# SSD scan of a hybrid encoder: y formed channel-major, carried states scaled by broadcast rows

## Chip, cores, metric

One core of a Trainium2 chip. The metric is the device time of one execution in microseconds (us). A lower time is better. The engines are TensorE (PE), VectorE (DVE), ScalarE (ACT), GpSimd (POOL) and SyncE (SP).

## What is computed

Two layers over 512 positions of width 1024 in float32: a bidirectional Mamba-2 SSD layer, then differential attention. The change lies in the scan of the first. It has 32 heads of 64 channels in 8 groups of 4 heads, a state of 128 per group, and 4 chunks of 128 positions:

```python
# per direction; xin = x * dt; C, B: (chunk, position, group, state)
L = where(lower triangle, exp(a_cs[l] - a_cs[s]), 0)
y_diag = einsum('bclgn,bcsgn,bgrcls,bcsgrp->bclgrp', C, B, L, X)
states = einsum('bcsgn,bgrcs,bcsgrp->bcgrpn', B, exp(a_cs[-1] - a_cs), X)
# scan over chunks: new = carry * exp(a_cs[-1]) + states; prev = the carry that each chunk receives
y_off = einsum('bclgn,bcgrpn,bgrcl->bclgrp', C, prev, exp(a_cs))
y = y_diag + y_off          # both directions are added, then
y = y + x * d_skip
y = rmsnorm(y * silu(z)) @ w_out
```

## The kernel before

The input projection is cut into units: one unit gives 128 output columns for all 512 positions, in 24 matmuls (`project`, L1290). Each iteration of the SSD stage has six slots, one unit each: slots 0 and 1 give z of scan group g, slots 2 and 3 give xT (the two 128-channel halves, two heads each), slot 4 BT and slot 5 CTr of group g + 1. Units alternate between banks 0 and 1, and `project` waits until the SiLU of the unit two before it is done (`silu_done`). Beside its unit, each slot carries a piece of the scan of group g. Groups 2 to 5 run in a hardware loop (two trips of two groups), the others are written out.

Every engine runs its instructions in the order written. The pieces for group g are, by slot:

- slot 0: PE transposes xT into banks 2 and 3 (L1309), ACT copies them to `x_nat` (position-major).
- slot 1: PE transposes BT and forms the products of B and C (bank 5). DVE forms the pair weights (`rows`, L967, L971): for each head and chunk the matrix of C, B and the decays of both directions.
- slot 2: PE forms the chunk states (L1333); DVE chains them into `prev` (L981, L987) and signals `prev_done`.
- slot 3: PE forms the within-chunk part: 16 matmuls per group with `rows` stationary and 64 columns of `x_nat` moving (L1344), then the part from the carried states: six matmuls with a chunk of CTr stationary and 256 columns of `prev` moving (L1357). DVE scales the second by `eacs` = exp(a_cs), one value per position (on partitions) and head (L1002), and adds both directions (L1008, L1011); y stands position-major in `x_nat`.
- slot 5: PE transposes y back to channels (L1364, eight 128x128 transposes); DVE adds the D skip (L1018), multiplies by the gate zT (L1021) and signals `g_done`.

In the last group, slot 3's carried-state work is spread over slots 3 and 4, and units of the output projection run in slots 2 to 5.

Within a slot DVE runs `conv` (four taps, L942), then the scan piece, then `silu` (L957), for slots 2 to 5. ACT runs, in a slot, `split_hi` of a later unit's weights (L612), `evacuate` (L654 or L650), scan copies and exponentials (L705), and `tanh` (L661) once `conv` is done. POOL forms `w_lo` (L471), masks `rows` (L503), scales x into `x_dec` (L492). SP loads the weights.

The order within a slot on DVE, which the change does not alter, is:

```python
                    if slot in slots and slot >= 2:
                        conv(m, half, slot)
                    if scan and slot < 5:
                        scan_ops(m * 2 + half, slot, half)
                    if slot in slots and slot >= 2:
                        silu(m, half, slot)
```

`Own` (L251) makes DVE wait for the instruction just issued, because the next one reads its result.

Of the kernel before, what the change touches and what calls it, by code (L numbers as in the profile page):

```python
# [23 lines left out]
F32 = mybir.dt.float32  # L24
# [99 lines left out]
def build(nc, x, norm_w, ssd_w_in, ssd_conv_w, ssd_conv_b, ssd_dt_bias, ssd_a_log, ssd_d,  # L124
# [3 lines left out]
    with stack:  # L128
# [3 lines left out]
        def sem(name):  # L132
# [30 lines left out]
        tmp = sb("tmp", [P, 2 * GW], F32, ssd)  # L163
        sq_acc = sb("sq_acc", [P, L], F32, ssd)
# [37 lines left out]
        acs_rows = nc.dram_tensor("acs_rows", (2 * HEADS, L), F32).ap()  # L202
        bias_rows = nc.dram_tensor("bias_rows", (AH, 2 * L), F32).ap()
# [22 lines left out]
        y_done, yt_done, g_done, sq_in, sq_done = (  # L226
            sem("y_done"), sem("yt_done"), sem("g_done"), sem("sq_in"), sem("sq_done"))
# [90 lines left out]
        def scan_banks(g):  # L318
# [18 lines left out]
        def load_rows(queue, g):  # L337

            after(queue, diag_done, g * 2)
# [9 lines left out]
        def _(sp):  # L349
# [37 lines left out]
            for n in range(UNITS_O1):  # L387
                if n == 8:
                    sp.wait_ge(diag_done, 2 * GROUPS)
# [214 lines left out]
        def _(act):  # L604
# [66 lines left out]
            def scan_ops(g, slot, half):  # L671
                if slot == 0:

                    after(act, y_done, g * NC)
                    after(act, yt_done, g * 2)
# [7 lines left out]
                if slot == 2:  # L683
                    act.wait_ge(st_done, g * 3 + 1)
                    after(act, off_done, g * NC)
                    nc.scalar.copy(pair(0), bank[scan_banks(g)[0][0]][:, :]).then_inc(prev0_in, 1)
# [65 lines left out]
            nc.scalar.activation(flat(eacs), flat(acs), ACT.Exp).then_inc(sp_a, 1)  # L752
# [134 lines left out]
        def _(dve):  # L887
# [85 lines left out]
            def scan_ops(g, slot, half):  # L973
                if slot == 2:

                    after(dve, off_done, g * NC)
                    after(dve, y_done, g * NC)
                    dve.wait_ge(prev0_in, g + 1)
                    state = scan_banks(g)[0]
# [12 lines left out]
                if slot == 3 or slot == 4 and last_g:  # L992

                    for c in (range(NC) if not last_g else range(2) if slot == 3 else range(2, NC)):
                        d0, d1 = (1 if c == 0 else 0), (1 if c == NC - 1 else 2)
                        if c == 0:
                            dve.wait_ge(prev_done, g + 1)
                        else:
                            dve.wait_ge(y_done, g * NC + c)
                        dve.wait_ge(off_done, g * NC + c + 1)  # L1000
                        dve.wait_ge(diag_done, g * 2 + c // 2 + 1)
                        own(V.tensor_tensor(  # L1002
                            tmp[:, d0 * GW:d1 * GW].rearrange("p (d r n) -> p d r n", d=d1 - d0, r=HPG),
                            bank[scan_banks(g)[1][c]][:, d0 * GW:d1 * GW].rearrange("p (d r n) -> p d r n", d=d1 - d0, r=HPG),
                            eacs[:, c, d0:d1, ds(g * HPG, HPG)].unsqueeze(3)
                            .to_broadcast([P, d1 - d0, HPG, HD]), ALU.mult))
                        within = bank[6 + c // 2][:, (c % 2) * GW:(c % 2 + 1) * GW]
                        ins = V.tensor_tensor(x_nat[:, c, :], within, tmp[:, d0 * GW:(d0 + 1) * GW], ALU.add)  # L1008
                        if d1 - d0 == 2:
                            own(ins)  # L1010
                            ins = V.tensor_tensor(x_nat[:, c, :], x_nat[:, c, :], tmp[:, GW:2 * GW], ALU.add)  # L1011
                        ins.then_inc(y_done, 1)
                if slot == 5:

                    for j in range(2):
                        t = gT_flat[:, ds((g * 2 + j) * L, L)]
                        dve.wait_ge(yt_done, g * 2 + j + 1)
                        own(V.scalar_tensor_tensor(bank[6 + j][:, :], xT[:, half, j, :],  # L1018
                                                   par[:, ds(g * 2 + (PC_D + j), 1)], bank[6 + j][:, :],
                                                   ALU.mult, ALU.add))  # L1020
                        V.tensor_tensor(t, bank[6 + j][:, :], zT[:, j, :], ALU.mult).then_inc(g_done, 1)  # L1021
# [7 lines left out]
            def ssd_iteration(m, half, slots=range(SLOTS), scan=True):  # L1029
                for slot in range(SLOTS):  # L1030
# [18 lines left out]
                    if scan and slot == 5:  # L1049
                        scan_ops(m * 2 + half, slot, half)  # L1050
# [9 lines left out]
            dve.wait_ge(sp_a, 7)  # L1060
# [10 lines left out]
            OWN_V = 2 * (4 * (TAPS - 2) + 2 + 3 + 6 + 2)  # L1071
# [549 lines left out]
```

## Time and profile before

| | us |
|---|---|
| median of 3 runs | 892.61 (891.35 to 892.84) |
| the profiled execution | 891.45 |
| its span | 889.7 |

| engine | busy us | share of the span |
|---|---|---|
| PE | 793.6 | 89% |
| PE weight load | 641.8 | 72% |
| DVE | 562.5 | 63% |
| POOL | 476.5 | 54% |
| ACT | 404.5 | 45% |

The SSD stage lies from about 40 to 460 us of the span, the scan groups 0 to 7 from about 60 to 445. Behind them come the output projection, the attention heads and the last projection, which the change does not touch. The profile names a line (L1261 is the line of the projections' matmul, inside a helper), an engine, an operation, and what it writes and reads. Matmuls of plain float32 operands appear as two records each. A duration of a matmul includes its latency: neighbours overlap, so their cost is read from start to start.

### The profile page before, as it was taken

The numbers are of one execution on the slowest core, as the hardware profiler recorded it, in microseconds if no ns is written. First come the engines' busy times: TensorE is split into PE (matmuls) and PEld (weight loads), VectorE is DVE, ScalarE is ACT, GpSimd is POOL, SyncE is SP. The second block draws the span as 40 slices with busy tenths as digits, with TensorE's granted clock in tenths as the row PEclk, the third lists the DMA queues.
The fourth block names the chain that finished last, engine by engine and source line by source line (L and its number), as shares of the span: only waits on it lengthen the run. The fifth ranks groups of instructions, "written<-read, shape, count | busy, mean of one in ns | idle before, by whom it ended". The sixth has DMA issues, their size and how long they took to land.

```text
span 889.7 us, 11512 instructions
## 1 busy us (share of the span) xinstructions
PE 793.6 (89%) x3824; PEld 641.8 (72%) x3824; DVE 562.5 (63%) x885; ACT 404.5 (45%) x807; POOL 476.5 (54%) x270
## 2 busy tenths in 40 slices
PE   1988999999999999997999998989888797987787
PEld 1767888878888787886878886766666575766566
DVE  4755878785969596876620134667676867667643
ACT  4556473727272645556322343545434363544330
POOL 5439584947484757575454447536353554536121
PEclk9999999999999999999999999999999999999899
DMA  8133534342424233341523233232122212120002
GB/s 256 48 116 106 165 95 143 90 148 69 161 56 139 80 93 136 94 144 48 189 89 111 76 106 100 72 92 62 54 69 66 67 55 68 47 91 24 1 0 95
DMA packets 98772, 82.70 MB, mean 93 GB/s; under 512 B 4992, under 2 KB 87392, under 8 KB 96680
## 3 DMA queue, kind: packets, MB, share of 16 engines
q1 hardware_dynamic: 95728, 67.12, 25.2%
q10 hardware_dynamic: 2904, 15.01, 4.6%
q8 instruction: 24, 0.39, 0.2%
q14 instruction: 20, 0.16, 0.1%
q0 software_dynamic: 96, 0.02, 0.0%
HBM read 79.87 MB, written 2.26 MB: 92 GB/s over the span
## 4 chain that ended last, share of the span: by engine, by line
PE 46%; DVE 27%; issue 13%; ACT 6%; POOL 6%; DVEq 1%; DMA 1%; ACTq 0%; SPq 0%; POOLq 0%
PE bank L1261 39%; DVE c_acc L942 5%; DVE rows L967 4%; POOL stat L463 3%; DVE qkvz L1170 2%; DVE sbias L1131 2%; DVE tmp L1002 2%; ACT rows L705 1%; DVE x_nat L1011 1%; DVE x_nat L1008 1%; PE bank L1478 1%; DVE tmp L981 1%; DVE rows L971 1%; ACT ex L801 1%; DVE rows L903 1%
## 5 line engine op out<-in xcount | busy, mean ns | idle before, releaser
L471 POOL TENSOR_TENSOR w_lo<-w_raw,w_hi 128x1024 fp32r<-128x1024 f32 x104 | 261.9, 2520 | 226.5 <-ACT w_hi L612 226.3
L1261 PE MATMUL bank<-hn_hi,w_hi 128*128 128x512 f32 (+1 forms) x392 | 160.7, 410 | 11.6 <-DVE xT L957 8.9
L1261 PE MATMUL bank<-hn_hi,w_lo 128*128 128x512 f32 (+1 forms) x392 | 155.5, 397 | 0.0
L1261 PE MATMUL bank<-hn_lo,w_hi 128*128 128x512 f32 (+1 forms) x392 | 154.8, 395 | 0.0
L612 ACT CAST w_hi<-w_raw 128x1024 fp32r<-128x1024 f32 x104 | 108.7, 1046 | 74.8 <-PE bank L1261 68.7
L1261 PE MATMUL bank<-w_hi,hn_hi 128*128 128x512 f32 x320 | 134.3, 420 | 6.9 <-DVE zT L957 5.0
L1261 PE MATMUL bank<-w_hi,hn_lo 128*128 128x512 f32 x320 | 127.9, 400 | 0.0
L1261 PE MATMUL bank<-w_lo,hn_hi 128*128 128x512 f32 x320 | 127.8, 399 | 0.0
L801 ACT ACTIVATE ex<-sbias,stat 128x512 f32<-128x512 f32 x64 | 45.7, 715 | 159.1 <-DVE stat L1135 159.1
L942 DVE SCALAR_TENSOR_TENSOR c_acc<-bank,par,c_acc 128x510 f32<-128x510 f32 (+1 forms) x128 | 95.8, 748 | 32.0 <-ACT c_acc L654 23.3
L1261 PEld LDWEIGHTS bank<-hn_hi,w_hi 128*128 128x128 f32 (+1 forms) x392 | 74.5, 190 | 30.2 <-issue 15.2
L503 POOL TENSOR_TENSOR rows<-rows,below 128x1024 f32<-128x1024 f32 x32 | 76.6, 2420 | 23.1 <-DMA rows<-acs_rows 23.1
L1261 PEld LDWEIGHTS bank<-hn_hi,w_lo 128*128 128x128 f32 (+1 forms) x392 | 74.2, 189 | 16.8
L1261 PEld LDWEIGHTS bank<-hn_lo,w_hi 128*128 128x128 f32 (+1 forms) x392 | 74.6, 190 | 15.3
L1261 PEld LDWEIGHTS bank<-w_hi,hn_hi 128*128 128x128 f32 x320 | 62.3, 195 | 27.1 <-issue 10.6
L705 ACT ACTIVATE rows<-rows,da 128x128 f32<-128x128 f32 x256 | 78.0, 393 | 3.2 <-POOL rows L503 3.2
L661 ACT ACTIVATE bank<-c_acc 128x512 f32<-128x512 f32 x32 | 19.3, 602 | 119.2 <-DVE c_acc L942 119.2
L1261 PEld LDWEIGHTS bank<-w_hi,hn_lo 128*128 128x128 f32 x320 | 61.8, 193 | 13.8
L1261 PEld LDWEIGHTS bank<-w_lo,hn_hi 128*128 128x128 f32 x320 | 62.5, 195 | 11.5
L1261 PE MATMUL bank<-w_hi,oT_hi 128*128 128x512 f32 x128 | 52.5, 410 | 3.0 <-DVE oT_lo L1220 1.4
L967 DVE TENSOR_TENSOR rows<-rows 128x512 f32<-128x512 f32 x32 | 51.2, 1633 | 2.9 <-ACT rows L705 2.9
L463 POOL TENSOR_TENSOR stat<-stat,expo 128x16 f32<-128x16 f32 (+1 forms) x16 | 31.3, 1953 | 36.7 <-DVE stat L1181 19.0
(193 smaller groups left out, 1319.2 us busy)
## 6 DMA issues: line engine op xcount, KB each, us to landing
w_raw<-in_ssd_w_in SPq DMA_DIRECT2D x48, 512.0 KB, 4.0
w_raw<-in_attn_w_in SPq DMA_DIRECT2D x64, 256.0 KB, 3.1
rows<-acs_rows ACTq DMA_DIRECT2D x14, 1024.0 KB, 6.5
w_raw<-in_ssd_w_out SPq DMA_DIRECT2D x16, 512.0 KB, 3.6
w_raw<-in_attn_w_out SPq DMA_DIRECT2D x16, 256.0 KB, 3.1
wbias<-bias_rows SPq DMA_DIRECT2D x8, 448.0 KB, 4.1
rows<-in_x SPq DMA_DIRECT2D x4, 512.0 KB, 5.3
rows<-acs_rows SPq DMA_DIRECT2D x2, 1024.0 KB, 5.7
```

Source lines behind the costliest of these rows:

```text
L463: return nc.gpsimd.tensor_tensor(dst, src, expo[:, 0:n], ALU.pow)
L471: nc.gpsimd.tensor_tensor(w_lo[:, s, :], w_raw[:, s, :], f32(w_hi[:, s, :]), ALU.subtract)\
L503: nc.gpsimd.tensor_tensor(pair_, pair_, below[:, :, :].unsqueeze(2).to_broadcast([P, 2, NC, P]), ALU.add).then_inc(mask_done, 1)
L612: nc.scalar.copy(w_hi[:, s, :], w_raw[:, s, :]).then_inc(hi_done, 1)
L661: nc.scalar.activation(bank[u.c % 2][:, :], c_acc[:, u.c % 2, :], ACT.Tanh).then_inc(tan_done, 1)
L705: ins = nc.scalar.activation(part, part, ACT.Exp, bias=da[:, c, d, ds(g * HPG + r, 1)])
L801: nc.scalar.activation(ex[:, j, :], sbias[:, j, :], ACT.Exp, bias=stat[:, 36 + j:37 + j], accum_out=stat[:, 40 + j:41 + j]).then_inc(e_don ...
L942: ins = V.scalar_tensor_tensor(c_acc[:, p, lo:hi], bank[p][:, lo + sh:hi + sh], par[:, ds(t + (PC_W + k * CT), 1)], c_acc[:, p, lo:hi], AL ...
L967: ins = V.tensor_tensor(rows[:, r, :], rows[:, r, :], rows[:, HPG + r, :], ALU.add)
L1002: own(V.tensor_tensor(tmp[:, d0 * GW:d1 * GW].rearrange("p (d r n) -> p d r n", d=d1 - d0, r=HPG), bank[scan_banks(g)[1][c]][:, d0 * GW:d1 ...
L1131: ins = V.tensor_tensor_reduce(out=sbias[:, j, :], in0=bank[4 + j][:, :], in1=w, scale=1.0, scalar=-3.0e38, op0=ALU.add, op1=ALU.max, accu ...
L1261: ins = T.matmul(dst, a[i], b[j], start=first and n == 0, stop=last and n == 2)
```

## The change

The within-chunk part is formed channel-major: `x_nat` (64 channels of a head) is stationary and `rows` (128 positions) moves; the two heads of a half go to partitions 0 to 63 and 64 to 127 of bank 6 or 7. The carried-state part has `prev` stationary (128 channels) and a chunk of CTr moving, so it also comes out channel-major, 384 columns for each direction and half. exp(a_cs) must then vary along columns: ACT forms it once as rows, writes it to DRAM (`exp_rows`) and loads it for each group, broadcast to 64 partitions a head (`edec`, two transfers of 512 KB). The eight y transposes go, and `y_done` and `yt_done` with them. DVE's work on y, the D skip and the gate stand together in slot 4; in the last group, in slots 3 and 4.

```diff
+        edec = sb("edec", [P, 2, 2, L], F32, ssd)
...
+        exp_rows = nc.dram_tensor("exp_rows", (2, HEADS, L), F32).ap()
...
+        def off_part(g, n):
             if isinstance(g, int) and g == GROUPS - 1:
-                return (4, 6, 7), (4, 5, 4, 5)
-            return (4, 2, 3), (2, 3, 4, 5)
+                return n // 2, n % 2, bank[4 + n % 2]
+            return n % 2, n // 2, bank[(2, 4, 3, 5)[n]]
+
+        def off_cols(d):
+
+            return slice(P, L) if d == 0 else slice(0, L - P)
...
             def scan_ops(g, slot, half):
                 if slot == 0:
 
-                    after(act, y_done, g * NC)
-                    after(act, yt_done, g * 2)
+                    after(act, diag_done, g * 4)
...
+            def load_decay(g):
+
+                after(act, g_done, g * 2)
+                if isinstance(g, int) and g == 0:
+                    act.wait_ge(erows_out, 32)
+                for i in range(2):
+                    act.dma_start(edec[i * HD:(i + 1) * HD, :, :, :].rearrange("p j d l -> p (j d) l"),
+                                  exp_rows[i][ds(g * 4, 4), :].partition_broadcast(HD)).then_inc(edec_in, 16)
...
                     if scan and slot == 1 and not (isinstance(m, int) and m * 2 + half == 0):
                         squares(m * 2 + half - 1)
+                    if scan and slot == 1:
+                        load_decay(m * 2 + half)
...
-            nc.scalar.activation(flat(eacs), flat(acs), ACT.Exp).then_inc(sp_a, 1)
...
+            nc.scalar.activation(sq[0:2 * HEADS, 0, :], bank[5][0:2 * HEADS, :], ACT.Exp).then_inc(erows_sb, 1)
             act.wait_ge(rows_sb, 1)
             act.dma_start(acs_rows, tmp[0:2 * HEADS, :]).then_inc(rows_out, 16)
+            act.wait_ge(erows_sb, 1)
+            for d in range(2):
+                act.dma_start(exp_rows.rearrange("i (q d) l -> d q i l", d=2)[d],
+                              sq[d * HEADS:(d + 1) * HEADS, 0, :]).then_inc(erows_out, 16)
...
-                if slot == 3 or slot == 4 and last_g:
-
-                    for c in (range(NC) if not last_g else range(2) if slot == 3 else range(2, NC)):
...
-                if slot == 5:
-
                     for j in range(2):
...
+                if slot == 4 and not last_g:
+                    for j in range(2):
+                        from_states(g, 2 * j, tmp)
+                        from_states(g, 2 * j + 1, c_tan)
+                        within(g, j, half)
+                        add_states(g, 2 * j, tmp)
+                        add_states(g, 2 * j + 1, c_tan)
+                        gated(g, j)
+
+            def from_states(g, n, dst):
+
+                d, j, b = off_part(g, n)
+                cols = off_cols(d)
+                dve.wait_ge(edec_in, g * 32 + 32)
+                dve.wait_ge(off_done, g * 4 + n + 1)
+                V.tensor_tensor(dst[:, cols], b[:, cols], edec[:, j, d, cols], ALU.mult).then_inc(off_used, 1)
+
+            def within(g, j, half):
+
+                dve.wait_ge(diag_done, g * 4 + 2 * j + 2)
+                own(V.scalar_tensor_tensor(bank[6 + j][:, :], xT[:, half, j, :], par[:, ds(g * 2 + (PC_D + j), 1)],
+                                           bank[6 + j][:, :], ALU.mult, ALU.add))
+
+            def add_states(g, n, src):
+
+                d, j, _ = off_part(g, n)
+                cols = off_cols(d)
+                dve.wait_ge(off_used, g * 4 + n + 1)
+                own(V.tensor_tensor(bank[6 + j][:, cols], bank[6 + j][:, cols], src[:, cols], ALU.add))
+
+            def gated(g, j):
+
+                V.tensor_tensor(gT_flat[:, ds((g * 2 + j) * L, L)], bank[6 + j][:, :], zT[:, j, :], ALU.mult)\
+                    .then_inc(g_done, 1)
...
                     if slot in slots and slot >= 2:
                         silu(m, half, slot)
-                    if scan and slot == 5:
-                        scan_ops(m * 2 + half, slot, half)
...
                 if slot == 0:
 
                     pe.wait_ge(silu_done, g * SLOTS + 2)
-                    after(pe, y_done, g * NC)
+                    after(pe, off_used, g * 4)
...
                     pe.wait_ge(m_done, g * HPG + HPG)
                     if last_g:
                         pe.wait_ge(prev_done, g + 1)
...
                     for j in range(2):
                         for c in range(NC):
-                            ins = T.transpose(bank[6 + j][:, c * P:(c + 1) * P], x_nat[:, c, j * P:(j + 1) * P],
-                                              ident[:, :])
-                        ins.then_inc(yt_done, 1)
+                            for i in range(2):
+                                r = 2 * j + i
+                                ins = T.matmul(bank[6 + j][i * HD:(i + 1) * HD, c * P:(c + 1) * P],
+                                               x_nat[:, c, r * HD:(r + 1) * HD], rows[:, r, c * P:(c + 1) * P],
+                                               start=True, stop=True)
+                                if c == NC - 1:
+                                    ins.then_inc(diag_done, 1)
+                if slot == 3 or slot == 4 and last_g:
+
+                    pe.wait_ge(prev_done, g + 1)
+                    for n in range(4) if not last_g else range(2) if slot == 3 else range(2, 4):
+                        d, j, b = off_part(g, n)
+                        if slot == 4:
+                            pe.wait_ge(off_used, g * 4 + n - 1)
+                        for k in range(3):
+                            c = (k + 1, 2 - k)[d]
+                            ins = T.matmul(b[:, c * P:(c + 1) * P], prev[:, k, d, j * P:(j + 1) * P],
+                                           CTr[:, c * P:(c + 1) * P], start=True, stop=True)
+                        ins.then_inc(off_done, 1)
```

## Rows read from the trace of the kernel before

**Rows 1.** The page: busy us (share of the span) and instructions by engine.

```profile
PE 793.6 (89%) x3824; PEld 641.8 (72%) x3824; DVE 562.5 (63%) x885; ACT 404.5 (45%) x807; POOL 476.5 (54%) x270
```

**Rows 2.** The waits: engine, line, what it waited for; us in total, times, longest us.

```profile
PE bank L1261 <- DVE xT L957: 8.9, 7, 2.4
```

**Rows 3.** The timeline of PE, scan group 3: start us, us, engine, line, operation, count, idle before.

```profile
203.65 0.47 PE L1261 MATMUL bank<-hn_hi,w_hi 128*128 128x512 f32 x1
...
230.46 3.68 PE L1344 MATMUL bank<-x_nat,rows 128*128 128x64 f32 x32
233.97 2.81 PE L1357 MATMUL bank<-prev,CTr 128*128 128x256 f32 x12
236.43 0.58 PE L1261 MATMUL bank<-hn_hi,w_hi 128*128 128x512 f32 x1
...
243.57 0.47 PE L1261 MATMUL bank<-hn_hi,w_hi 128*128 128x512 f32 x1 [1.30 <-DVE xT L957]
...
249.14 1.03 PE L1364 MATMUL bank<-ident,x_nat 128*128 128x128 f32 x8
249.93 0.47 PE L1261 MATMUL bank<-hn_hi,w_hi 128*128 128x512 f32 x1
```

**Rows 4.** Stretch of slot 4's projection: length, busy us (count) by engine, clock, DMA.

```profile
236.43:242.11 5.68, 5.68 (x26) 4.49 (x24) 5.01 (x10) 1.65 (x2) 2.52 (x1) 1.00 0.98 342
```

**Rows 5.** The timeline of DVE, scan group 3.

```profile
232.11 0.69 DVE L987 TENSOR_TENSOR prev<-tmp,bank 128x512 f32<-128x512 f32 x1
...
236.66 0.41 DVE L1002 TENSOR_TENSOR tmp<-bank,eacs 128x256 f32<-128x256 f32 x1
...
242.74 0.68 DVE L957 SCALAR_TENSOR_TENSOR xT<-bank,c_acc 128x512 f32<-128x512 f32 x1
243.38 3.43 DVE L942 SCALAR_TENSOR_TENSOR c_acc<-bank,par,c_acc 128x510 f32<-128x510 f32 x4
```

**Rows 6.** The timeline of PE in attention: two matmuls of 64 rows each.

```profile
645.21 0.51 PE L1261 MATMUL bank<-qT_hi 64*128 64x512 f32 x2
```

**Rows 7.** The timeline of PE, last scan group, after its longest wait.

```profile
408.69 0.79 PE L1261 MATMUL bank<-w_hi,hn_hi 128*128 128x512 f32 x1 [4.96 <-DVE zT L957]
...
410.13 0.63 PE L1261 MATMUL bank<-w_hi,hn_hi 128*128 128x512 f32 x1
...
415.45 0.39 PE L1261 MATMUL bank<-w_hi,hn_lo 128*128 128x512 f32 x1
```

**Rows 8.** Groups by line and shape: count | busy us, mean ns | idle before.

```profile
L1002 DVE TENSOR_TENSOR tmp<-bank,eacs 128x512 f32<-128x512 f32 x16 | 11.1, 691 | 5.0 <-issue 3.3 <-DVE x_nat L1011 0.9
...
L1002 DVE TENSOR_TENSOR tmp<-bank,eacs 128x256 f32<-128x256 f32 x16 | 6.7, 420 | 3.1 <-PE bank L1357 2.4
```

**Rows 9.** The timeline of DVE: D skip and gate, in the loop, then written out.

```profile
208.84 0.75 DVE L1018 SCALAR_TENSOR_TENSOR bank<-xT,par,bank 128x512 f32<-128x512 f32 x1
209.73 0.69 DVE L1021 TENSOR_TENSOR gT<-bank,zT 128x512 f32 x1
...
394.93 0.74 DVE L1018 SCALAR_TENSOR_TENSOR bank<-xT,par,bank 128x512 f32<-128x512 f32 x1
395.71 0.69 DVE L1021 TENSOR_TENSOR gT<-bank,zT 128x512 f32<-128x512 f32 x1
```

**Rows 10.** The timeline of ACT, slot 4 of scan group 3.

```profile
242.46 0.78 ACT L654 ACTIVATE c_acc<-bank,par 128x512 f32<-128x512 f32 x1 [3.54 <-PE bank L1261]
```

**Rows 11.** The timelines of ACT's queue and of PE ahead of the first scan group.

```profile
58.63 0.55 ACTq L759 DMA_DIRECT2D acs_rows<-tmp  x1
...
82.48 2.86 PE L1333 MATMUL bank<-x_dec,B_nat 128*128 128x256 f32 x12 [3.02 <-POOL x_dec L492]
```

**Rows 12.** The timeline of PE: slot 4 of group 0, slot 0 of groups 1 and 7.

```profile
96.64 0.58 PE L1261 MATMUL bank<-hn_hi,w_hi 128*128 128x512 f32 x1
...
108.98 0.47 PE L1261 MATMUL bank<-hn_hi,w_hi 128*128 128x512 f32 x1
...
390.33 0.47 PE L1261 MATMUL bank<-hn_hi,w_hi 128*128 128x512 f32 x1
```

More of the change, by code:

```diff
@@ L337, in load_rows @@
         def load_rows(queue, g):
-            after(queue, diag_done, g * 2)
+            after(queue, diag_done, g * 4)
             if isinstance(g, int) and g == 0:
@@ L684, in scan_ops @@
                     act.wait_ge(st_done, g * 3 + 1)
-                    after(act, off_done, g * NC)
-                    nc.scalar.copy(pair(0), bank[scan_banks(g)[0][0]][:, :]).then_inc(prev0_in, 1)
+                    after(act, off_done, g * 4)
+                    nc.scalar.copy(pair(0), bank[state_banks(g)[0]][:, :]).then_inc(prev0_in, 1)
                 first = isinstance(g, int) and g == 0
@@ L974, in scan_ops @@
                 if slot == 2:
-                    after(dve, off_done, g * NC)
-                    after(dve, y_done, g * NC)
+                    after(dve, off_done, g * 4)
                     dve.wait_ge(prev0_in, g + 1)
-                    state = scan_banks(g)[0]
+                    state = state_banks(g)
                     for k in range(2):
@@ L991, in scan_ops @@
                 last_g = isinstance(g, int) and g == GROUPS - 1
-                if slot == 3 or slot == 4 and last_g:
-                    for c in (range(NC) if not last_g else range(2) if slot == 3 else range(2, NC)):
[L995 to L1012, printed above, removed]
@@ L1013, in scan_ops @@
-                if slot == 5:
-                    for j in range(2):
[L1016 to L1021, printed above, removed]
+                if slot == 3 and last_g:
+                    for j in range(2):
+                        from_states(g, j, (tmp, c_tan)[j])
+                    for j in range(2):
+                        within(g, j, half)
+                        add_states(g, j, (tmp, c_tan)[j])
@@ new lines, in scan_ops @@
+                if slot == 4 and last_g:
+                    for j in range(2):
+                        from_states(g, 2 + j, (tmp, c_tan)[j])
+                    for j in range(2):
+                        add_states(g, 2 + j, (tmp, c_tan)[j])
+                        gated(g, j)
+                if slot == 4 and not last_g:
+                    for j in range(2):
+                        from_states(g, 2 * j, tmp)
+                        from_states(g, 2 * j + 1, c_tan)
+                        within(g, j, half)
+                        add_states(g, 2 * j, tmp)
+                        add_states(g, 2 * j + 1, c_tan)
+                        gated(g, j)
@@ L1330, in scan_ops @@
                     for k in range(3):
-                        b = bank[scan_banks(g)[0][k]]
+                        b = bank[state_banks(g)[k]]
                         for d, (c, i) in enumerate(((k, k), (3 - k, 2 - k))):
@@ L1340, in scan_ops @@
                         pe.wait_ge(prev_done, g + 1)
-                    for c in range(NC):
-                        for r in range(HPG):
-                            at = (c % 2) * GW + r * HD
-                            ins = T.matmul(bank[6 + c // 2][:, at:at + HD], rows[:, r, c * P:(c + 1) * P],
-                                           x_nat[:, c, r * HD:(r + 1) * HD], start=True, stop=True)
-                        if c % 2:
-                            ins.then_inc(diag_done, 1)
+                    for j in range(2):
+                        for c in range(NC):
+                            for i in range(2):
[5 more added lines that the diff above has]
+                                    ins.then_inc(diag_done, 1)
@@ L1348, in scan_ops @@
                 if slot == 3 or slot == 4 and last_g:
                     pe.wait_ge(prev_done, g + 1)
-                    for c in (range(NC) if not last_g else range(2) if slot == 3 else range(2, NC)):
+                    for n in range(4) if not last_g else range(2) if slot == 3 else range(2, 4):
+                        d, j, b = off_part(g, n)
                         if slot == 4:
-                            pe.wait_ge(y_done, g * NC + c - 1)
-                        for d in range(2):
-                            k = (c - 1, 2 - c)[d]
-                            if 0 <= k < 3:
-                                ins = T.matmul(bank[scan_banks(g)[1][c]][:, d * GW:(d + 1) * GW], CTr[:, c * P:(c + 1) * P],
-                                               prev[:, k, d, :], start=True, stop=True)
-                        ins.then_inc(off_done, 1)
@@ L1360, in scan_ops @@
-                if slot == 5:
-                    pe.wait_ge(y_done, g * NC + NC)
-                    for j in range(2):
-                        for c in range(NC):
-                            ins = T.transpose(bank[6 + j][:, c * P:(c + 1) * P], x_nat[:, c, j * P:(j + 1) * P],
-                                              ident[:, :])
-                        ins.then_inc(yt_done, 1)
+                            pe.wait_ge(off_used, g * 4 + n - 1)
[3 more added lines that the diff above has]
+                                           CTr[:, c * P:(c + 1) * P], start=True, stop=True)
```

20 lines of the change are left out of this document (11 added, 9 removed).

## Prediction

> **What bounds the kernel now.** I read the page first: TensorE (PE) is busy 89% of the span, far ahead of VectorE (DVE) at 63% [rows 1]. A change that takes eight transposes a group off PE should therefore pay, unless it makes PE wait. So the second view is the list of waits: in the scan stage PE hardly waits, and its repeated wait is for DVE's SiLU of xT, 8.9 us in 7 times, the longest 2.4 [rows 2]. That wait shows the rule that decides here. `project` of a unit waits for `silu_done` of the unit two before it, because they share bank 0 or 1. In a slot DVE runs conv, then the scan work of that slot, then the SiLU, so scan work delays the release of the bank.
>
> Third, the timeline of PE over one trip of the loop (scan group 3), and those of DVE and ACT beside it. PE begins slot 0 at 203.65; within-chunk products run from 230.46, the products with carried states from 233.97, slot 4 from 236.43, slot 5 from 243.57, the y transposes from 249.14, and the next slot 0 starts at 249.93: a period of 46.28 us [rows 3]. Slot 4's projection takes 5.68 us, to 242.11 [rows 4]; so PE waits some 1.4 us before slot 5. DVE shows why: its y work of slot 3 starts at 236.66 and only at 242.74 does it reach the SiLU of slot 3; PE starts 0.83 us later [rows 3, 5]. This block sits in the slot where PE has most other work: between the ends of projections 3 and 4 it also has 5.97 us of scan products [rows 3], which hide nearly the whole block. In slot 4 DVE then has only the conv, from 243.38 [rows 5], and its SiLU, done well before PE wants bank 0 at 249.93. The remaining four instructions on y stand after the SiLU of slot 5 and delay no projection that is close.
>
> **Off PE.** The eight y transposes cost 249.14 to 249.93, 0.79 us a group [rows 3], 6.3 us in all. They matter only where PE is the last to be ready; after the change slot 0 waits for DVE (below), so in seven groups this is worth nothing and in the last 0.8 us.
>
> **Carried states on PE.** Six matmuls of 256 columns become twelve of 128: 1,536 columns either way. I take the same 2.46 us [rows 3].
>
> **Within-chunk products on PE.** Sixteen matmuls, each now with 64 stationary and 128 moving columns, two heads into the two halves of the output partitions. Today's take 3.51 us in 32 records, 0.110 each [rows 3]. The trace has no column halves. The nearest row is the one of row halves in the attention stage: two 64-row matmuls of 512 columns together cover 0.51 us, where one alone is recorded with 0.39, so they ran side by side [rows 6, 7]. If column halves do that too, the 16 matmuls cost half, about 1.8 us; if each waits for the other, some 3.4; if every change of half also cost the 0.11 by which slot 4's projection, which follows matmuls of another form, is longer than slot 5's [rows 3, 4], 5.2. I take 1.8, nearest to the only row with two halves. Not all of the 1.7 gained counts in the loop: the carried-state products also wait for `prev_done`, whose last instruction starts at 232.11 and takes 0.69 [rows 5], so they can start near 232.95 in place of 233.97: 1.0 us in each of the four groups in the loop, by my estimate up to 1.65 in the three written out, where DVE is faster, and 1.7 in the last. Sum: about 10 us.
>
> The Trainium skill, "TensorEngine Tiling (Array Packing)", section "Key Properties", says that different tiles run weight loads and matmuls in parallel. Its page "TensorE: Matmul & The Clock Gate", section "The mechanism", speaks against this change: there a weight load overlaps running matmuls only when the row group differs, and the two column halves have the same rows. By the first the products cost about 1.8 us, by the second about 3.4; the two matmuls of [rows 6] have different rows and so can't choose between them.
>
> **DVE's work on y.** Before, per group: four multiplications (two of 512 columns at 691 ns, two of 256 at 420 [rows 8]), six additions of 256, then twice a D-skip and a gating. After: four multiplications and four additions of 384 columns, and the same D-skips and gatings. 384 columns lie between the two forms, 0.555 us. What matters is that all twelve now stand in one block in slot 4 (groups 0 to 6), ahead of the SiLU of slot 4. Its length: an instruction that only follows another starts about 0.08 before the recorded end of the first, one that waits for its own result later. In the loop the D-skip starts at 208.84 and its gating at 209.73, so 0.89; written out, 394.93 and 395.71, so 0.78 [rows 9]. Per half of the channels, in the loop: two multiplications 2 x 0.55, D-skip 0.89, two additions with such waits 2 x 0.70, gating 0.65: 4.04, so 8.1 for the block. Written out: 2 x 0.50 + 0.78 + 2 x 0.60 + 0.61 = 3.6, so 7.2. An addition that reads and writes PSUM is not in the trace; the D-skip does both, in 0.75 for 512 columns, which bounds it, and nothing makes it cheaper than the 0.42 that a 256-column multiplication takes [rows 8, 9]: the block lies between 6.3 and 9.
>
> **The new path from the end of projection 4 to the next slot 0.** ACT evacuates from 242.46, an evacuation takes some 0.8, so DVE's conv of slot 4 starts no earlier than 243.2 (1.1 us behind PE's 242.11) and takes 3.43, 3.36 to the start of the next instruction. Then come the block, 8.1, and the SiLU with PE's start, 0.83 [rows 5, 10]. Sum 13.4 us in the loop and 12.1 where the code is written out (its three waits inside the conv are each 0.11 shorter, as 0.89 against 0.78 [rows 9]). PE itself has only slot 5's projection, 5.57 us, to do in that time [rows 3]: it stands still some 7 us in each of groups 0 to 6. Nothing hides this, since PE runs its projections in order. DVE is meanwhile idle from the SiLU of slot 3, about 238.1, until conv 4. The stall of 1.4 us ahead of slot 5 goes, but what is late next is later still. DVE's conv of slot 5 and ACT's tanh and exps behind it are also pushed back, but by as much as PE's next slot 0, so they add nothing.
>
> **The clock.** The wait of 4.96 us at 408.69 is followed by a unit that starts at half the clock: instructions of 0.63 in place of 0.39, and its 24th matmul starts at 415.45; with one more step of 0.23 the unit took 6.99 us, where 5.57 is usual [rows 3, 7]. A 7 us wait should do the same in each of seven iterations: +1.42 us each.
>
> **Added transfers.** ACT issues two broadcasts of 512 KB a group in slot 1, behind the squares, and waits for `g_done`, which the squares wait for as well. Two issues hold ACT's queue for about 1 us, at 0.55 for the one at 58.63 [rows 11], ahead of the split and evacuation of slot 2. I cost them at nothing, since DVE is then still at the pair weights of slot 1 and PE at the projection of slot 2; without that cover they would be 1 us a group, 8 in all. The data is first read in slot 4, more than 20 us on. Ahead of the first group ACT gets one more exponential of 64x512 and two issues, each like the 0.55 at 58.63 [rows 11], and loses one smaller exponential: some +1.4 us. PE's wait of 3.02 at 82.48 for POOL's x_dec [rows 11] hangs on this chain through the split weights, so I count it whole.
>
> **The sum.** Slot 0 of groups 1 and 7 start at 108.98 and 390.33: six periods of 46.9 on average [rows 12]. New period without a gain from column halves: 38.46 (203.65 to 242.11) + 1.42 + 13.4 = 53.3 in the four groups of the loop, 38.46 + 1.42 + 12.1 = 52.0 in the two written out. 4 x 53.3 + 2 x 52.0 = 317.2, less 281.35: +35.8. Group 0 begins slot 4 at 96.64: 96.64 + 5.68 + 12.1 = 114.4 against 108.98, +5.4 [rows 12]. Last group: +1.42 - 0.79 = +0.6. Ahead of the scan +1.4. Together +43.2. Column halves give back 10: +33.2. The profiled execution took 891.45 (span 889.7), 1.2 below the median of 892.61; 891.45 + 33.2 = 924.7, and on the median 925.8. I forecast 926.
>
> **The rivals.**
> Column halves take turns: everything else stands, 892.6 + 43.2 = 936. For it: today the products are paced by something other than 64 moving columns, since 0.110 a record of 64 columns is more than the 0.099 of a transpose of 128 (0.79 for eight [rows 3]). Against: [rows 6]. Chance 0.33.
> The stall is there but cheaper: half clock in only some iterations, or a block of 6.3: 917 to 922. Chance 0.07.
> Dearer than both: additions into PSUM at 9 us a block, or a settling time at each change of half, 941 to 950. Chance 0.07.
> Faster: the cut on PE decides. This needs the DVE block in slot 4 to be short enough to hide under slot 5's projection. The point is a block of about 4.2 us: 37.4 to the end of projection 4, 5.3 around the block, 46.9 today. If it were wholly hidden, transposes 6.3, stalls 8.9 [rows 2] and column halves 13.6 would go and 1.4 come: 865. Against: twelve instructions in 4.2 us are 0.35 each, and even 256 columns take 0.42 [rows 8]. Faster 0.02, no difference 0.01.
> My forecast has 0.50. Two measurements of this kernel can't be told apart below about 0.2%, 1.8 us. So faster 0.02, same 0.01, slower 0.97. The range 917 to 941 takes in the second and third case and most doubt on the block.
>
> **What would show it.** PE's waits should name DVE's SiLU of BT (slot 4) with about 7 us, seven times, and no longer xT. Slot 0 should begin with 0.63 us matmuls. The DVE timeline should show 7 to 8 us of y work between conv and SiLU of slot 4. The within-chunk products should take 1.8 us and the carried ones start right behind `prev_done`. I am wrong if DVE's block is under 4 us, if slot 0 starts within a microsecond of the end of slot 5, or if the attention stage changes length at all.

## The result, and the profile after

| | before | after |
|---|---|---|
| median, us | 892.35 (891.35 to 892.84) | 925.94 (923.53 to 926.24) |
| profiled execution, us | 891.45 | 926.24 |
| its span, us | 889.7 | 923.9 |

The changed kernel is slower: ratio 1.0372, with a 95% interval of 1.0352 to 1.0392. The page of after: its busy times, where [rows 1] stand for before, and its row of granted clock in tenths, with that of before below it:

```profile
PE 791.4 (86%) x3856; PEld 634.1 (69%) x3856; DVE 529.0 (57%) x869; ACT 406.2 (44%) x807; POOL 469.6 (51%) x270
...
PEclk9998999898989899898899999999999999998899
```

```profile
PEclk9999999999999999999999999999999999999899
```

PE does as much as before, 791.4 us against 793.6, in a span that is 34.2 us longer. DVE even lost 33.5 us of busy time. So the engines did not get more to do; PE stood still. The row of the clock only hints at it, with an 8 in every second or third slice of the scan, since a slice averages over 23 us. The list of waits names for whom PE stood still (columns as in [rows 2]):

```profile
PE bank L1299 <- DVE BT L982: 49.4, 8, 7.1
```

Before, the repeated wait was for xT, 8.9 us [rows 2]. Now it is for the SiLU of BT, slot 4. Seven of the eight waits, of 6.2 to 7.1 us, stand ahead of slot 0 of groups 1 to 7; the eighth, 2.3 us, stands ahead of group 0, where before has one of 2.6. The timeline of PE in scan group 3, to be read beside [rows 3]:

```profile
218.19 0.77 PE L1299 MATMUL bank<-hn_hi,w_hi 128*128 128x512 f32 x1 [7.11 <-DVE BT L982]
...
246.81 1.97 PE L1383 MATMUL bank<-rows,x_nat 128*64 128x128 f32 x32
248.70 2.94 PE L1397 MATMUL bank<-CTr,prev 128*128 128x128 f32 x24
251.40 0.48 PE L1299 MATMUL bank<-hn_hi,w_hi 128*128 128x512 f32 x1
...
269.57 0.80 PE L1299 MATMUL bank<-hn_hi,w_hi 128*128 128x512 f32 x1 [7.00 <-DVE BT L982]
270.16 0.63 PE L1299 MATMUL bank<-hn_lo,w_hi 128*128 128x512 f32 x1
...
276.80 1.03 PE L1347 MATMUL bank<-ident,xT 128*128 128x128 f32 x8
```

Slot 0 starts at 218.19 and again at 269.57: 51.38 us, where [rows 3] have 46.28. Up to slot 4 the group hardly got longer: 33.21 us from slot 0 to slot 4, against 32.78. Slot 4 begins at 251.40, its projection ends near 257.0, slot 5's near 262.6, and then PE waits 7.00 us. When it starts again its matmuls last 0.63 instead of 0.39: the granted clock was 0.5 there, its lower level of 1.2 GHz, and slot 0's projection takes 7.23 us up to the next transposes, where 5.57 is usual [rows 3]. DVE shows what PE waits for (as [rows 5]):

```profile
245.81 0.69 DVE L1011 TENSOR_TENSOR prev<-tmp,bank 128x512 f32<-128x512 f32 x1
...
252.09 0.69 DVE L982 SCALAR_TENSOR_TENSOR xT<-bank,c_acc 128x512 f32<-128x512 f32 x1 [0.67 <-ACT bank L672]
258.24 3.43 DVE L967 SCALAR_TENSOR_TENSOR c_acc<-bank,par,c_acc 128x510 f32<-128x510 f32 x4 [5.45 <-ACT c_acc L665]
261.58 0.55 DVE L1043 TENSOR_TENSOR tmp<-bank,edec 128x384 f32<-128x384 f32 x1
262.05 0.55 DVE L1043 TENSOR_TENSOR c_tan<-bank,edec 128x384 f32<-128x384 f32 x1
262.51 0.75 DVE L1048 SCALAR_TENSOR_TENSOR bank<-xT,par,bank 128x512 f32<-128x512 f32 x1
263.29 0.56 DVE L1056 TENSOR_TENSOR bank<-bank,tmp 128x384 f32<-128x384 f32 x1
263.89 0.57 DVE L1056 TENSOR_TENSOR bank<-bank,c_tan 128x384 f32<-128x384 f32 x1
264.60 0.69 DVE L1060 TENSOR_TENSOR gT<-bank,zT 128x512 f32 x1
...
268.83 0.68 DVE L982 SCALAR_TENSOR_TENSOR BT<-bank,c_acc 128x512 f32<-128x512 f32 x1
```

After the SiLU of slot 3 DVE sits idle for 5.45 us. The conv of slot 4 follows at 258.24, then the block on y from 261.58 to 268.83, and only then the SiLU of BT.

The two profiled executions differ by 34.8 us, their spans by 34.2. Where those lie: slot 0 of group 1 starts at 115.98 and that of group 7 at 422.71, where [rows 12] have 108.98 and 390.33. So 7.0 came up to group 1, 25.4 in the six periods behind it, 0.1 in the last group. The last 1.7 arose in the attention stage, where nothing changed:

```profile
582.73 1.10 PE L1546 MATMUL bank<-ident,qkvz 128*128 128x128 f32 x8 [2.96 <-DVE qkvz L1210]
583.58 0.68 PE L1299 MATMUL bank<-w_hi,hn_hi 128*128 128x512 f32 x1
584.06 0.63 PE L1299 MATMUL bank<-w_lo,hn_hi 128*128 128x512 f32 x1
```

PE's matmuls run there at half clock for one projection, behind transposes that had waited 2.96 us. Before has the same wait, 2.95 us, and full clock behind it:

```profile
550.13 1.09 PE L1513 MATMUL bank<-ident,qkvz 128*128 128x128 f32 x8 [2.95 <-DVE qkvz L1172]
550.98 0.47 PE L1261 MATMUL bank<-w_hi,hn_hi 128*128 128x512 f32 x1
```

Of the twelve traces of this document, nine have the slow stretch at this place, about 1.6 us long, and three have none (before, the old form in slot 4, the squares one slot later). The whole part behind the SSD stage, which no version alters, takes between 427.6 and 431.8 us in these traces. What decides whether the slow stretch comes stays open. So this 1.7 is not shown to come from the change.

### The profile page after: what moved, and what is told of

The parts are those of the page before. It is cut to its first block, busy times and chain, and to the rows that moved or that the text cites. A ratio compares the mean times of both kernels' runs of the same rounds, so it can differ in the third digit from the quotient of the medians.

```text
span 923.9 us, 11598 instructions
## 1 busy us (share of the span) xinstructions
PE 791.4 (86%) x3856; PEld 634.1 (69%) x3856; DVE 529.0 (57%) x869; ACT 406.2 (44%) x807; POOL 469.6 (51%) x270
## 4 chain that ended last, share of the span: by engine, by line
PE 56%; DVE 19%; issue 12%; POOL 7%; ACT 4%; DMA 1%; DVEq 1%; ACTq 0%; SPq 0%; POOLq 0%
PE bank L1299 46%; DVE c_acc L967 3%; PE bank L1397 2%; POOL stat L474 2%; PE bank L1371 2%; DVE qkvz L1208 2%; DVE sbias L1169 2%; DVE bank L1056 2%; PE bank L1383 2%; DVE bank L1048 1%; POOL rows L514 1%; ACT ex L826 1%; DVE aT_lo L1186 1%; DVE rows L928 1%; POOL gate L586 1%
## 5 line engine op out<-in xcount | busy, mean ns | idle before, releaser
L482 POOL TENSOR_TENSOR w_lo<-w_raw,w_hi 128x1024 fp32r<-128x1024 f32 x104 | 258.9, 2492 | 262.8 <-ACT w_hi L623 262.5
L1299 PE MATMUL bank<-hn_hi,w_hi 128*128 128x512 f32 (+1 forms) x392 | 163.8, 418 | 52.0 <-DVE BT L982 49.4
L1299 PE MATMUL bank<-hn_lo,w_hi 128*128 128x512 f32 (+1 forms) x392 | 157.9, 403 | 0.0
L1299 PE MATMUL bank<-hn_hi,w_lo 128*128 128x512 f32 (+1 forms) x392 | 157.7, 402 | 0.0
L967 DVE SCALAR_TENSOR_TENSOR c_acc<-bank,par,c_acc 128x510 f32<-128x510 f32 (+1 forms) x128 | 95.8, 749 | 68.8 <-ACT c_acc L665 60.1
L1299 PEld LDWEIGHTS bank<-hn_hi,w_hi 128*128 128x128 f32 (+1 forms) x392 | 76.9, 196 | 71.7 <-issue 41.8
L1299 PEld LDWEIGHTS bank<-hn_hi,w_lo 128*128 128x128 f32 (+1 forms) x392 | 76.3, 195 | 17.7
L1299 PEld LDWEIGHTS bank<-hn_lo,w_hi 128*128 128x128 f32 (+1 forms) x392 | 77.0, 196 | 15.9
L1299 PE MATMUL bank<-w_lo,oT_hi 128*128 128x512 f32 x128 | 51.7, 404 | 0.0
L1299 PE MATMUL bank<-w_hi,oT_lo 128*128 128x512 f32 x128 | 51.5, 402 | 0.0
```

The lines of the kernel that those rows point to most:

```text
L482: nc.gpsimd.tensor_tensor(w_lo[:, s, :], w_raw[:, s, :], f32(w_hi[:, s, :]), ALU.subtract)\
L967: ins = V.scalar_tensor_tensor(c_acc[:, p, lo:hi], bank[p][:, lo + sh:hi + sh], par[:, ds(t + (PC_W + k * CT), 1)], c_acc[:, p, lo:hi], AL ...
L1299: ins = T.matmul(dst, a[i], b[j], start=first and n == 0, stop=last and n == 2)
```

## The experiments

My theory was that the loss comes from the place of DVE's block: between the last scan products and the release of bank 0, with one more piece of PE work to hide it. Rivals were the new matmul forms and the broadcast transfers. Each kernel was timed beside the kernel before (in three series, with medians of 892.7, 892.5 and 894.0 us for it).

**The y block in slot 3.** Only the order on DVE is edited; `half_y` is one half's scaling, D skip and additions, and the rest of the change stays:

```diff
-                if slot == 4 and not last_g:
-                    for j in range(2):
...
+                    if scan and slot == 3 and not last_g:
+                        half_y(m * 2 + half, 0, half)
+                    if scan and slot == 5 and not last_g:
+                        gated(m * 2 + half, 0)
+                        gated(m * 2 + half, 1)
                     if slot in slots and slot >= 2:
                         silu(m, half, slot)
+                    if scan and slot == 3 and not last_g:
+                        half_y(m * 2 + half, 1, half)
```

> The changed kernel with DVE's work on y moved in groups 0 to 6: the first half of the channels between conv and SiLU of slot 3, the second half behind the SiLU of slot 3, both gatings between conv and SiLU of slot 5. Matmuls, transfers and the last group stay. Theory (the place of the block makes the loss): from the end of projection 4 to slot 0 the path is 1.1 + 3.4 + 0.7 + 0.7 + 0.15 = 6.0 us, against 12.5 now, and slot 0 runs at full clock; period 37.1 + 6.0 = 43.1, against 51.1; seven times 8 us off: about 870. If the new matmul forms or the broadcast transfers make the loss: 915 or more. If DVE becomes the bound in slots 0 to 2: 875 to 890.

Measured: 880.03 us, ratio 0.986 (0.9802 to 0.9917). With the same matmuls and transfers the kernel is now a little faster than the one before, so the place is what made the loss. The 870 was missed by 10. PE, group 3:

```profile
229.33 2.94 PE L1403 MATMUL bank<-CTr,prev 128*128 128x128 f32 x24 [0.78 <-DVE prev L1011]
...
244.70 0.50 PE L1305 MATMUL bank<-hn_hi,w_hi 128*128 128x512 f32 x1 [1.51 <-DVE BT L982]
```

PE waits 0.78 for `prev_done` (up to 2.0 in other groups) and 1.5 ahead of slot 0; the period is 45.0, not 43.1. DVE's chain now holds PE up at two places, as the third expectation had it.

**The SiLU of slot 4 first.**

```diff
+                    if slot == 4 and slot in slots:
+                        silu(m, half, slot)
                     if scan and slot < 5:
                         scan_ops(m * 2 + half, slot, half)
-                    if slot in slots and slot >= 2:
+                    if slot in slots and slot >= 2 and slot != 4:
```

> The changed kernel with one swap: the SiLU of slot 4 ahead of the y block of slot 4. Theory (any 7 us block on DVE behind the last scan products ends up ahead of some SiLU that PE needs): bank 0 is free in time, but conv and SiLU of slot 5 come 7 us late, and PE waits some 5.5 us before slot 1 for bank 1, again at half the clock: 918 to 925, nearly no gain. Rival (only bank 0's release matters): the wait goes and does not come back, 870 to 885.

Measured: 921.56 us, ratio 1.0336 (1.0277 to 1.0394). The wait moved by one unit, as expected:

```profile
PE bank L1301 <- DVE CTr L982: 37.8, 8, 5.4
```

It is now for CTr, slot 5, up to 5.4 us. To free bank 0 earlier is no cure if the block then delays bank 1.

**Slot 5's projection twice.**

```diff
-                for k in range(KT):
+                twice = slot == 5 and not (isinstance(m, int) and m < 0)
+                for k in list(range(KT)) * (2 if twice else 1):
```

> The changed kernel with slot 5's projection run twice into the same bank (the second pass starts the sum anew, so the result is that of one pass): 24 more matmuls, 5.5 us more PE work in each iteration, put into PE's wait. Theory (the wait is DVE's, and its second cost is the half clock behind it): the wait shrinks to about 1.5 us, slot 0 starts where it did but at full clock, 1.7 us saved in each of seven iterations: about 914, faster with more work. If the clock cost nothing: 926. If PE were the bound: 7 x 5.5 more, 965.

Measured: 910.61 us, ratio 1.022 (1.0162 to 1.0278), 3.4 below the 914 expected. With 168 more matmuls, 38 us at full clock, the kernel is 15 us faster than the change. PE's waits for BT fell from 49.4 us to

```profile
PE bank L1299 <- DVE BT L982: 11.4, 8, 2.3
```

and behind them no projection starts slowly; slot 0 of group 4:

```profile
264.51 0.50 PE L1299 MATMUL bank<-hn_hi,w_hi 128*128 128x512 f32 x1 [1.57 <-DVE BT L982]
264.85 0.39 PE L1299 MATMUL bank<-hn_lo,w_hi 128*128 128x512 f32 x1
```

Half clock is left in the scan groups 1 to 7 only behind the wait of 5.0 us for zT in the last, which before has too [rows 7]. So PE's wait costs twice: its length, and the slow start behind it. Of the 16.0 us between the two spans, 11.6 have been gained when slot 0 of group 7 is done, 1.65 for each of seven groups, near the 1.7 expected. 4.1 lie in the untouched part behind the SSD stage and say nothing of the edit.

**The block shorter.** Only the two gatings leave slot 4, for slot 5 between conv and SiLU (the `gated` lines of the first diff).

> The changed kernel with the two gatings alone taken out of slot 4's block and put between conv and SiLU of slot 5. Theory (PE's wait is the length of the block, one for one): the block shortens from 7.2 to 6.0 us, seven times 1.2: 917.5. Rival (the wait is set by something else on the way, the transfers or ACT): 924 to 926.

Measured: 920.59 us, ratio 1.0306 (1.0267 to 1.0345): 5.3 us less than the change, not 8.4. PE, slot 0 of groups 3 and 4:

```profile
213.89 0.77 PE L1301 MATMUL bank<-hn_hi,w_hi 128*128 128x512 f32 x1 [5.78 <-DVE BT L982]
...
222.06 1.04 PE L1349 MATMUL bank<-ident,xT 128*128 128x128 f32 x8
...
264.86 0.79 PE L1301 MATMUL bank<-hn_hi,w_hi 128*128 128x512 f32 x1 [5.69 <-DVE BT L982]
```

The wait did shrink one for one, 7.00 to 5.69. But slot 0's projection now takes 8.17 us (213.89 to 222.06) against 7.27 in after (218.19 to 225.46), since its half-clock stretch lasts longer. The period falls by 0.4, not 1.3. My sum had treated the clock's price as fixed.

**Order by halves, and one half only.** First the order of the loops, then the output rows:

```diff
-                        for c in range(NC):
-                            for i in range(2):
+                        for i in range(2):
+                            for c in range(NC):
```

> The changed kernel with the 16 within-chunk matmuls in another order: for each pair of heads first the four of one head (partitions 0 to 63), then the four of the other, so that neighbours in the order no longer use different column halves. Theory (two column halves run side by side when they alternate): 32 records take 3.3 to 3.5 us instead of 1.9, on PE's path in all eight groups, +1.4 to 1.6 each: 937 to 939. Rival (1.9 us comes from the narrower weight loads, not from overlap): 926.

Measured: 932.11 us, ratio 1.0456 (1.0398 to 1.0513). The matmuls' group (busy us, mean ns):

```profile
L1383 PE MATMUL bank<-rows,x_nat 128*64 128x128 f32 x256 | 20.5, 279 | 0.0
```

In after it is 15.7 busy (below). The order alone costs time, so alternating halves do overlap; but it is a miss in size, 2.6 us a group rather than 3.3 to 3.5. The next kernel asks whether overlap or the narrower weights made up the rest:

```diff
-                                ins = T.matmul(bank[6 + j][i * HD:(i + 1) * HD, c * P:(c + 1) * P],
+                                ins = T.matmul(bank[6 + j][0:HD, c * P:(c + 1) * P],
```

> The changed kernel with all 16 within-chunk matmuls writing partitions 0 to 63 (the heads meant for partitions 64 to 127 overwrite the others, so the output differs). No two neighbours use different column halves. If alternating halves overlap: the 32 records take longer than the 2.50 us of the order by halves, at most 3.4: 932 to 939. If the 2.50 us had nothing to do with overlap: 932 again; if alternation is worth nothing at all: 926.

Measured: 941.98 us, ratio 1.055 (1.0518 to 1.0582), a little above the range that I gave.

```profile
L1383 PE MATMUL bank<-rows,x_nat 128*64 128x128 f32 x256 | 29.7, 274 | 0.0
```

29.7 us over eight groups is 3.7 us a group, 0.116 a record; alternating halves take half of that. The weights are as narrow here, so they are not what makes the change's order fast: the halves run side by side. Runs of four matmuls in one half take a third less than 3.7; how, these traces don't show. They could overlap at the changes of half, or part of the 3.7 could come from neighbours that now write the same columns of the bank, which no run here separates.

**The old form in the new place.** The kernel before, with `slot == 3` and `slot == 4` exchanged in the condition of DVE's scaling and adding, so that groups 0 to 6 do it in slot 4:

> The kernel before, with one edit: in groups 0 to 6 DVE's scaling and adding of y (6.1 us) stands in slot 4 instead of slot 3, where the change put its block. No new matmul form, no transfer, the y transposes stay. Theory (the place alone makes the loss): from the end of projection 4 to slot 0 it takes 1.1 + 3.4 + 6.1 + 0.8 = 11.4 us instead of 7.8, and slot 0 runs at half clock: about 4.7 us a period, +30 to 36: 922 to 929. Rival (the new forms or the broadcast rows are to blame): 893.

Measured: 943.98 us, ratio 1.058 (1.0555 to 1.0604). The sign is right: the place alone makes a loss, without new forms or transfers. But it is 15 us above my range. PE (group 2 and slot 0 of group 3), then DVE (group 3):

```profile
206.43 0.58 PE L1261 MATMUL bank<-hn_hi,w_hi 128*128 128x512 f32 x1
...
224.69 1.97 PE L1364 MATMUL bank<-ident,x_nat 128*128 128x128 f32 x8 [6.97 <-DVE x_nat L1008]
226.31 0.78 PE L1261 MATMUL bank<-hn_hi,w_hi 128*128 128x512 f32 x1
```

```profile
273.38 2.21 DVE L1011 TENSOR_TENSOR x_nat<-x_nat,tmp 128x256 f32<-128x256 f32 x1
```

From the end of slot 4's projection, 212.1, to slot 0 at 226.31 it takes 14.2 us, not 11.4. Two prices were left out. The y transposes can't start before all of y is done, so they stand behind the wait, and at half clock they take 1.6 instead of 0.79. And the additions of `x_nat` and `tmp` (L1011, 0.42 us at their shortest) take up to 2.21 us here, so that the block takes 7.8, not 6.1. The change's block of 7.25 is the better form for that place; it is the place that is wrong.

**No later transfers.**

```diff
-                for i in range(2):
+                for i in range(2 if isinstance(g, int) and g == 0 else 0):
...
-                dve.wait_ge(edec_in, g * 32 + 32)
+                dve.wait_ge(edec_in, 32)
```

> The changed kernel without the broadcast loads of exp rows in groups 1 to 7 (it scales with group 0's rows, so the output differs). Theory: the 8.4 MB and their issue on ACT's queue cost nothing, since nobody waits for them: 924 to 927. Rival (they take DMA time from the weights, or hold ACT up by 1 us a group): 917 or less.

Measured: 923.78 us, ratio 1.0346 (1.0329 to 1.0363), 2 us below after and at the edge of what can be told from nothing. The scan did not gain it: slot 0 of group 7 starts at 424.71, later than the 422.71 of after. PE's wait did not move:

```profile
PE bank L1299 <- DVE BT L982: 49.4, 8, 7.1
```

**Two steps further.** The version with y in slot 3, with the second half's additions behind the conv of slot 5 and the gatings behind the SiLU of slot 5:

> The version with y split over slot 3 (880 us), with the two additions of the second half moved behind the conv of slot 5 and the gatings behind the SiLU of slot 5. There the second part of the block held the conv of slot 4 up by about 1.1 us and PE waited 1.5 us before slot 0. Theory (PE waits for DVE's chain of slot 4): conv 4 starts as soon as it is evacuated, 1.1 us off each of seven groups: 872 to 874. Rival (DVE's pair weights in slot 1, slowed beside POOL, are the bound): 878 to 880.

Measured: 877.63 us, ratio 0.9851 (0.9819 to 0.9883), not told apart from 880.03 and above the 872 to 874 of the theory. In group 3 PE's wait ahead of slot 0 fell to 0.52, but its wait for `prev_done` rose to 1.94, and from 6.3 to 7.6 us over all groups: the rival. DVE in slot 1 of group 3, and POOL beside it:

```profile
211.24 3.52 DVE L992 TENSOR_TENSOR rows<-rows 128x512 f32<-128x512 f32 x2
214.79 1.28 DVE L996 TENSOR_TENSOR rows<-rows,bank 128x512 f32<-128x512 f32 x2
215.99 4.10 DVE L992 TENSOR_TENSOR rows<-rows 128x512 f32<-128x512 f32 x2
```

```profile
211.21 2.40 POOL L482 TENSOR_TENSOR w_lo<-w_raw,w_hi 128x1024 fp32r<-128x1024 f32 x1
215.49 2.36 POOL L482 TENSOR_TENSOR w_lo<-w_raw,w_hi 128x1024 fp32r<-128x1024 f32 x1 [1.88 <-ACT w_hi L623]
217.81 1.73 POOL L521 TENSOR_TENSOR sq_acc<-sq_acc,sq 128x512 f32<-128x512 f32 x1
```

The additions of `rows` (L992, two at a time) take 3.52 and 4.10 us. POOL works during the first 2.4 us of the one pair and through nearly the whole of the other. In after POOL was idle from 233.0 to 237.5, and each pair took 1.29, the second and POOL's next instruction being:

```profile
235.79 1.29 DVE L992 TENSOR_TENSOR rows<-rows 128x512 f32<-128x512 f32 x2
```

```profile
237.54 2.38 POOL L482 TENSOR_TENSOR w_lo<-w_raw,w_hi 128x1024 fp32r<-128x1024 f32 x1 [4.52 <-ACT w_hi L623]
```

Last, POOL's squares one slot later:

```diff
-                    if scan and slot == 2 and not (isinstance(m, int) and m * 2 + half == 0):
+                    if scan and slot == 3 and not (isinstance(m, int) and m * 2 + half == 0):
```

> The further split version (878 us) with POOL's two additions into the sum of squares moved from slot 2 to slot 3. There DVE's second pair of additions of rows (both operands and result in SBUF) took 4.10 us beside POOL's w_lo and squares, while the changed kernel took 1.29 for it with POOL idle, and PE waited 1.94 us for prev_done. Theory (these additions are slow only while POOL runs): without the squares beside it the pair takes about 3 us, prev_done comes 1.1 us earlier, 870 us. Rival (their length has another cause, or DVE's chain is not what PE waits for): 877 to 878.

Measured: 872.09 us, ratio 0.9763 (0.9724 to 0.9802), the fastest version, 2.4% below the kernel before and near the theory's 870. PE's waits for `prev_done` fell from 7.6 to 4.4 us, and the second pair took 1.1 us less:

```profile
215.37 3.00 DVE L992 TENSOR_TENSOR rows<-rows 128x512 f32<-128x512 f32 x2
```

## Why the prediction was right, and where it was off

The mechanism was right. The forecast was 926, measured 925.94, but that the two agree so closely is luck: errors cancel, as the sums below show. By its own steps:

- **Where PE would wait.** Right, and with it the sign: for BT, seven times 6.2 to 7.1 us, each followed by 0.63 us matmuls. The place was shown to be the cause by three kernels (y in slot 3, SiLU first, old form in the new place).
- **The block.** 8.1 us in the loop was too long: it took 7.25 (261.58 to 268.83). The error is 0.41 a half. The two multiplications make 0.17 of it: they start 0.46 to 0.47 apart, where I took 0.55, nearly their whole duration. Then the waits in the loop, for which I had carried over the 0.89 from D skip to gating [rows 9]: here the D skip at 262.51 is followed at 263.29, 0.78, and the additions by 0.60 and 0.71 (0.70 each forecast); the gating takes 0.61, not 0.65. The path from slot 4's projection to slot 0 was 12.5, not 13.4. Additions into PSUM take 566 ns, 18 more than the multiplications of 384 columns.
- **Column halves.** 1.8 forecast, 1.89 measured, side by side as taken from [rows 6]. The Trainium skill's "TensorEngine Tiling (Array Packing)", section "Key Properties", by which different tiles work in parallel, agrees with this trace, 1.89 against 3.7 with one half only; the remark in "TensorE: Matmul & The Clock Gate", section "The mechanism", on weight loads of the same row group did not keep the halves apart here. The kernel before already spoke against that remark: its projections start a matmul of all 128 rows every 0.23 us, and a weight load for the same rows takes 0.19 us of each such step, so loads do run beside matmuls of their own row group.
- **What they are worth.** I let `prev_done` cap the gain at 1.0 us in the loop. It did not: `prev` is complete near 246.5, before the within-chunk products even begin, and the carried products start at 248.70, right behind them. DVE's pair weights were faster than I assumed (below). Against that, the carried products take 2.70 in place of 2.46, which I had taken as unchanged: 1.4 us gained in all. My own terms add up to 10.65 over the kernel, which I rounded down to 10.
- **The clock.** 1.42 a period forecast, 1.7 measured, on average over the seven. Its price isn't fixed: with the gatings in slot 5, behind a wait of 5.78 us, it was 2.6 in group 3.
- **Ahead of the scan.** The states of group 0 start 1.55 later, as forecast, 1.4. But half clock then also covered them and the next projection, which I had not counted: the within-chunk products start at 93.93 instead of 90.67.

```profile
84.03 4.25 PE L1371 MATMUL bank<-x_dec,B_nat 128*128 128x256 f32 x12 [2.11 <-POOL x_dec L503]
...
93.93 0.77 PE L1383 MATMUL bank<-rows,x_nat 128*64 128x128 f32 x10
```

- **Transfers** at nothing: right within 2 us for groups 1 to 7.
- **Attention unchanged**: it got 1.7 us longer by one half-clock stretch, which by my own test would have proved me wrong. The same work varies by up to 4 us between the traces here, so the test was too strict.

The sums: six periods +25.4 where I had 28.5 after the halves' part, up to group 1 +7.0 where I had 5.2, last group +0.1 where I had -1.1, attention +1.7 where I had 0. Together that is 34.2 against 32.6 by my terms, one error of 3.1 one way and three of together 4.7 the other.

The groups of lines of after, for these terms (columns as in [rows 8]), and below them the line of before that answers to L992:

```profile
L992 DVE TENSOR_TENSOR rows<-rows 128x512 f32<-128x512 f32 x32 | 24.5, 801 | 3.0 <-ACT rows L724 3.0
...
L1397 PE MATMUL bank<-CTr,prev 128*128 128x128 f32 x192 | 23.7, 279 | 0.0
...
L1383 PE MATMUL bank<-rows,x_nat 128*64 128x128 f32 x256 | 15.7, 276 | 0.0
...
L1056 DVE TENSOR_TENSOR bank<-bank,tmp 128x384 f32<-128x384 f32 x16 | 9.1, 566 | 0.5
...
L1043 DVE TENSOR_TENSOR tmp<-bank,edec 128x384 f32<-128x384 f32 x16 | 8.8, 548 | 2.7 <-PE bank L1397 2.7
```

```profile
L967 DVE TENSOR_TENSOR rows<-rows 128x512 f32<-128x512 f32 x32 | 51.2, 1633 | 2.9 <-ACT rows L705 2.9
```

## What to carry to other kernels

Before moving work on a side engine, look for what it holds up in order: here a 7 us block made PE wait 7 us a period in one slot; split over slots 3 and 5, where matmuls covered most of it, it left 2.3 us. Count the cover on the bottleneck engine between the moment the block can start and the moment its successor is needed. Removing work from the bottleneck engine pays nothing where that engine is about to wait: here even 38 us more of work cost nothing there. A wait of 5 to 7 us brought a slow start besides.

## What was not expected of the hardware

DVE additions whose operands and result all lie in SBUF are slow beside POOL, and those that read PSUM are not. The Trainium skill states this rule in "SBUF — State Buffer", section "Who interferes with whom" (two SBUF inputs contend with a GpSimd instruction that reads SBUF); these traces agree, and I had not applied it to the change. L967 before took 1633 ns on average for 512 columns; the same instruction took 801 in after, 684 at the median, where POOL's w_lo and squares fell mostly beside other work; the multiplication that reads `bank` took 684 and 683. Shifting POOL's squares by one slot took 5.5 us off the kernel. So the wait of PE moved DVE and POOL apart: 26.7 us less of DVE time in L992 alone. The old form in slot 4, where PE waits too, has the same 801; with y in slot 3 the mean is back at 1676.

Idle time of PE was dearer than work: 24 matmuls without effect in each of the seven waits took 11.6 us off the scan.
